# Attention scores taken on all 128 rows of TensorE, and three value tiles joined into one run, in a two-block transformer kernel

## The chip, the cores and the metric

One core of one Trainium2 chip runs the whole program. The metric is the time of one execution on the device in microseconds. The kernel before was run three times: 2970.2, 2977.2 and 2979.04 us, with a median of 2977.2 us.

## The reference

Two transformer layers of one sequence of 256 tokens and 2048 features, in float32. What matters here are the attentions, whose heads have 64 features, half of the 128 rows of the memories and of the product array.

```
# first block: chunked attention, 16 heads
scores = einsum('bcqhd,bckhd->bhcqk', qc, kb) * (hd ** -0.5)
p = softmax(scores + bias, masked)
out = einsum('bhcqk,bckhd->bcqhd', p, vb)

# second block: four mixers of 8 heads: (a) dilated, (b) window with sink and 2 shared KV heads,
#   (c) block selection, (d) native sparse attention: compressed + selected + window branches, gated
o_cmp = einsum('bhgqn,bhnd->bhgqd', softmax(q @ kc), vc)      # 15 compressed keys
```

Around them stand the projections `x @ w_in`, a memory attention (4 heads of 256 features), a convolution, feed-forward layers and a mixture of 16 experts.

## The kernel before

Activations lie with features on the 128 partitions and tokens along the row, in `pool`, 75 slots of 256 columns. A slot of queries or keys holds two heads: one on rows 0 to 63 and one on rows 64 to 127. All weights come as 1 MB tiles of 128 x 2048. Each tile passes four engines: SyncE issues its DMA into `raw`, ScalarE rounds it to float32r (`w_hi`, line 582), VectorE takes the rest (`w_lo`, line 1846), and TensorE multiplies it with split activations, three products for each pair of chunks (`three`, lines 1155 to 1157, or `both`, lines 1168 and 1169). Four tiles are in flight.

TensorE's stream is written out by hand: tile by tile, and in two places the attention of one head at a time is put between half tiles. Each such piece is a tick. At tick u, `attend` issues the scores of unit u (line 1361; 1358 for compressed keys; 1352 for memory heads), the transposes of the probabilities of unit u-3 (lines 1372 to 1378), and the value products of unit u-4 (lines 1391 to 1399). VectorE, ScalarE and GpSimd do the softmax of unit u in their own streams: VectorE adds the bias and takes the maximum (1932), ScalarE takes the exponential (714), VectorE the reciprocal (1958), GpSimd scales (2585), and after the transposes ScalarE copies them from PSUM to SBUF (730). TensorE waits for that copy before it transposes the next unit into the same PSUM bank. Local ticks lie in the stage called "glu", five to four tiles.

The second block's projections are the list `SECOND`: tiles of kind "rows" (output has features on the partitions), "cmp" (the weights of the key and value compression, 30 moved columns), "tokens" (values with tokens on the partitions, one 128-wide tile: products of 128 moved columns), "quad" (four tiles of values at once, products of 512 moved columns) and "out". `SLOT2` says which half of `psT` a tile sums into. `tick_half` places the units: 8 sink units, then 8 heads of native sparse attention with three units each (two causal, one compressed), then twice 8 causal heads. `idle_products` are products of ones that keep TensorE's clock up while it has to wait.

Of the kernel before, what the change touches and what calls it, by code (L numbers as in the profile page):

```python
# [207 lines left out]


def second_tiles():  # L210

    out = [("rows", K2 + 9, 1.0), ("rows", V2 + 8, 1.0), ("rows", Q2 + 4, 0.125), ("cmp", 0, 0),
           ("rows", Q2 + 5, 0.125), ("cmp", 1, 0), ("rows", Q2 + 6, 0.125), ("rows", Q2 + 7, 0.125),
           ("rows", K2 + 8, 1.0), ("tokens", V2 + 9, 1.0)]
    out += [("rows", Q2 + 12 + c, 0.125) for c in range(4)]
    out += [("rows", K2 + 10, 1.0), ("rows", K2 + 11, 1.0), ("tokens", V2 + 10, 1.0), ("tokens", V2 + 11, 1.0)]
# [9 lines left out]
def second_slots():  # L226

    out, at = [], 0
    for kind, _, c in SECOND:
        out.append(at)  # L230
        at = at if kind == "quad" and c < 3 else 1 - at
    return out
# [87 lines left out]
def build(nc, tiles, ada_tiles, x_d, mem_d, params_d, crow_d, rel_rev, onehot_d, maskrow_d, ident_d,  # L320
          cmpmask_d, tab_d, sinks_d, rbias_d, router_d, gd_d, w2_d, pe_d, grp_d, tri_d, out, fbias_d):
    with ExitStack() as ctx:
# [22 lines left out]
        ident = sb("ident", [P, P])  # L345
        small = sb("small", [P, 880])
        rstd = sb("rstd", [P, S])
# [98 lines left out]
        zero = col(1)  # L446
        kc_sb = col(NCMP)
        vc_sb = col(P)[0:NCMP, :]
        rb, grp = col(NE), col(NE)
# [125 lines left out]
        def _(act):  # L575
# [126 lines left out]
            def attend(units, at, scratch, ticks=None):  # L702
                n = len(units)
                for u in range(n + 3) if ticks is None else ticks:
# [15 lines left out]
                    if u >= 3:  # L720
                        v = u - 3
                        unit, slot = units[v], (at + v) % 2
                        act.wait_ge(W["probs_transposed"], at + v + 1)
                        wait(act, W["pv_ready"], at + v - 1)
                        dst = flat(scratch[1] + 2 * slot, 2)
                        if unit["kind"] == "cmp":
                            ins = nc.scalar.activation(dst[0:NCMP, 0:S], psP[0:NCMP, 0:S], ACT.Copy)
                        else:
                            w = 2 * S if unit["kind"] == "mem" else S + P
                            ins = nc.scalar.activation(dst[:, 0:w], psP[:, 0:w], ACT.Copy)  # L730
                        ins.then_inc(W["probs_copied"], 1)
# [52 lines left out]
            linear("k", HC, K, 1.0)  # L784
            token_major("v", V)
# [212 lines left out]
            for n, (kind, dest, x) in enumerate(SECOND):  # L998
# [19 lines left out]
                attend(SECOND_UNITS, 20, SC2, ticks_at(n, 0, N_UNITS + 3))  # L1018
                if kind in ("rows", "tokens"):
                    act.wait_ge(used, t.count())  # L1020
                    nc.scalar.activation(pool[:, dest, :], psT[:, SLOT2[n], 0:S], ACT.Copy, scale=x)\
                        .then_inc(emptied["A"], 1)
                elif kind == "quad" and x == 3:
                    token_sums(t + -3, SLOT2[n], dest)
# [113 lines left out]
        def _(pe):  # L1138
# [201 lines left out]
            def attend(units, at, scratch, q0, k0, v0, outs, ticks=None):  # L1340
                n = len(units)
                for u in range(n + 4) if ticks is None else ticks:
                    if u < n:
                        unit, slot = units[u], (at + u) % 2

                        mem = u >= 2 and units[u - 2]["kind"] == "mem"
                        wait(pe, W["exp_ready"] if mem else W["max_ready"], at + u - 1)
                        for qt in range(2):
                            dst = psS[:, slot, qt * S:qt * S + S]
                            if unit["kind"] == "mem":  # L1350
                                for c in range(2):
# [12 lines left out]
                    if 3 <= u < n + 3:  # L1364
# [4 lines left out]
                        for qt in range(2):  # L1369
                            p = pool[:, scratch[0] + 2 * ((at + v) % 4) + qt, :]  # L1370
                            if unit["kind"] == "cmp":
                                last = nc.tensor.transpose(psP[0:NCMP, qt * P:qt * P + P], p[:, 0:NCMP], ident[:, :])
                                continue
                            last = nc.tensor.transpose(psP[:, qt * P:qt * P + P], p[:, 0:P], ident[:, :])
                            if unit["kind"] == "mem":
# [4 lines left out]
                    if u >= 4:  # L1380
# [178 lines left out]
            def second_half(n, half):  # L1559

                kind, what, x = SECOND[n]
                t = Tile(BASE["two"] + n)
                slot = SLOT2[n]
                if half == 0:
                    pe.wait_ge(lo_done, t.count())
                    before = slot_before(n)
                    if before is not None and not (kind == "quad" and x):
                        who = OWN[BASE["two"] + before]
                        pe.wait_ge(emptied[who], OWN[:BASE["two"] + before + 1].count(who))
# [22 lines left out]
                else:  # L1592
                    tt = half
                    for k in range(DC if kind == "tokens" else 4):
                        if kind == "tokens":
                            dst, kk, at, width = psT[:, slot, tt * P:tt * P + P], k, k * P, P
                        else:
                            dst, kk, at, width = psT[:, slot, tt * 512:tt * 512 + 512], 4 * x + k, 512 * k, 512
                        xh, xl = a_hi[:, kk, tt * P:tt * P + P], a_lo[:, kk, tt * P:tt * P + P]
                        wh, wl = w_hi[:, t.k % SPL, at:at + width], w_lo[:, t.k % SPL, at:at + width]  # L1600
                        nc.tensor.matmul(dst, xh, wh, start=kk == 0, stop=False)
# [5 lines left out]
            def second_ticks(n, half):  # L1607
# [4 lines left out]
                for u in ticks_at(n, half, N_UNITS + 4):  # L1612
                    if u in (0, 8, 32, 40):
                        pe.wait_ge(emptied["A"], OWN[:BASE["two"] + {0: 10, 8: 18, 32: 30, 40: 42}[u]].count("A"))
                    attend(SECOND_UNITS, 20, SC2, Q2, K2, V2, 20, [u])
# [31 lines left out]
            run_sums("norm2")  # L1647
            idle_products(14)
            pe.wait_ge(W["router_lo"], 1)
# [184 lines left out]
        def _(dve):  # L1834
# [144 lines left out]
            nc.vector.memset(ones[:, :], 1.0).then_inc(W["ones_set"], 1)  # L1979
            nc.vector.memset(zero, 0.0).then_inc(W["ones_set"], 1)  # L1980
            nc.vector.memset(g8, -3.0e38)
            nc.vector.memset(w8, -3.0e38).then_inc(W["ones_set"], 1)
# [65 lines left out]
            for n in range(HC):  # L2048
# [4 lines left out]
                attend(MEM_UNITS, 0, SC1, QM, mem_ticks(n, 1, 8))  # L2053
            joined("k", 2 * HC, K, 1.0)
            others("v", HC)
# [272 lines left out]
            def cmp_ready(r):  # L2328

                dve.wait_ge(W["cmp_out"], r + 1)  # L2330
                if r == 0:
                    for j in range(2):
                        ins = nc.vector.tensor_copy(kc_sb[64 * j:64 * j + 64, :],
                                                    psP[64 * j:64 * j + 64, NCMP * j:NCMP * j + NCMP])
                else:
                    ins = nc.vector.tensor_copy(vc_sb, psP[0:NCMP, 0:P])
                ins.then_inc(W["cmp_ready"], 1)
# [373 lines left out]
def layout(a):  # L2711
# [61 lines left out]
    second = cut(np.concatenate([part[10], part[11], heads(part[3]), part[4], part[5], heads(part[9]), part[12],  # L2773
                                 part[14], part[13], part[15]], axis=1), 16, 1)
    second = np.concatenate([second[0:3], cut(a["nsa_cmp_w1_k_2"][0], 16, 1), second[3:4],
# [54 lines left out]
```

## Time and profile before

| | |
|---|---|
| median of three runs | 2977.2 us |
| the profiled execution | 2975.78 us |
| its span, first to last instruction | 2973.7 us |
| TensorE busy | 2912.3 us, 98% |
| VectorE busy | 2166.5 us, 73% |
| ScalarE busy | 1493.1 us, 50% |
| mean granted clock of TensorE | 0.991 |

TensorE is busy nearly throughout. Matmuls are pipelined and their ends are modelled: a product that takes 0.28 us in the profile is followed by the next after 0.12 us. The granted clock has two levels, 1 (2.4 GHz) and 0.5 (1.2 GHz).

### The profile page before, as it was taken

To read this page: it belongs to the slowest core of one execution; us is meant where nothing else is said; L and a number is where in the kernel's file an instruction comes from. 1 tells how busy PE (TensorE), PEld (TensorE's weight loads), DVE (VectorE), ACT (ScalarE), POOL (GpSimd) and SP (SyncE) were. 2 spreads that over 40 slices of the span, in tenths; PEclk is the share of its full clock that TensorE was granted. 3 is DMA by queue.
4 is the path that set the end of the run, shared out by engine and by line. 5 is a ranking of instruction groups with operands and counts; after the bars stand their busy time and mean duration, and the time that the engine had idled before them with its cause. 6 is when DMAs were issued, how large, how long until landed. Compare 5 with 4: busy or idle time off the path is not lost.

```text
span 2973.7 us, 46205 instructions
## 1 busy us (share of the span) xinstructions
PE 2912.3 (98%) x18218; PEld 2604.1 (88%) x18218; DVE 2166.5 (73%) x2651; ACT 1493.1 (50%) x1691; POOL 158.3 (5%) x228
## 2 busy tenths in 40 slices
PE   9999999999999999999999989999999999999998
PEld 8888788888888899999999989988989889889887
DVE  5644459999876999999999864455765876776874
ACT  5543554445554544444444444445545664664663
POOL 3000000000000000000000200111110000000001
PEclk9999999999999999999999989999999999999999
DMA  7545445555554988887788564344406895885882
GB/s 277 185 155 184 164 147 191 185 183 184 205 195 155 360 333 319 332 331 314 318 327 329 216 217 170 135 152 154 135 28 231 334 345 222 316 334 213 341 311 83
DMA packets 114816, 692.27 MB, mean 233 GB/s; under 512 B 14144, under 2 KB 27696, under 8 KB 33648
## 3 DMA queue, kind: packets, MB, share of 16 engines
q1 hardware_dynamic: 109088, 675.33, 60.2%
q10 hardware_dynamic: 4688, 11.01, 1.2%
q0 software_dynamic: 896, 3.93, 0.4%
q8 instruction: 100, 1.64, 0.2%
q14 instruction: 44, 0.36, 0.0%
HBM read 679.74 MB, written 10.49 MB: 232 GB/s over the span
## 4 chain that ended last, share of the span: by engine, by line
PE 89%; DVE 5%; ACT 3%; issue 1%; DMA 1%; POOL 0%; DVEq 0%; ACTq 0%; SPq 0%; POOLq 0%
PE psT L1168 22%; PE psT L1169 11%; PE psT L1155 6%; PE psT L1156 6%; PE psT L1157 6%; PE psT L1277 3%; PE psT L1732 3%; PE psT L1730 3%; PE psT L1731 3%; PE psT L1720 2%; PE psT L1721 2%; PE psT L1719 2%; DVE w_lo L1846 2%; PE psY L1771 1%; PE psY L1769 1%; PE psY L1770 1%
## 5 line engine op out<-in xcount | busy, mean ns | idle before, releaser
L1846 DVE TENSOR_TENSOR w_lo<-raw,w_hi 128x2048 fp32r<-128x2048 f32 x534 | 1225.1, 2298 | 395.2 <-ACT w_hi L582 391.3
L582 ACT ACTIVATE w_hi<-raw 128x2048 fp32r<-128x2048 f32 x534 | 1019.0, 1909 | 399.5 <-PE psT L1157 139.4
L1168 PE MATMUL psT<-a_both,w_hi 128*128 128x512 f32 x3072 | 1091.0, 400 | 9.9 <-DVE a_both L1896 2.8
L1169 PE MATMUL psT<-a_both,w_lo 128*128 128x256 f32 x3072 | 864.6, 281 | 0.0
L1168 PEld LDWEIGHTS psT<-a_both,w_hi 128*128 128x128 f32 x3072 | 579.0, 188 | 152.8 <-issue 9.9
L1169 PEld LDWEIGHTS psT<-a_both,w_lo 128*128 128x128 f32 x3072 | 582.9, 190 | 0.2
L1155 PE MATMUL psT<-a_both,w_hi 128*128 128x256 f32 x784 | 228.6, 292 | 8.3 <-DVE w_lo L1846 5.6
L1155 PE MATMUL psT<-h_hi,w_hi 128*128 128x256 f32 (+1 forms) x800 | 228.7, 286 | 4.9 <-DVE h_lo L2310 1.8
L1157 PE MATMUL psT<-h_hi,w_lo 128*128 128x256 f32 (+1 forms) x800 | 227.8, 285 | 0.0
L1156 PE MATMUL psT<-h_lo,w_hi 128*128 128x256 f32 (+1 forms) x800 | 227.7, 285 | 0.0
L1156 PE MATMUL psT<-a_both,w_hi 128*128 128x256 f32 x784 | 224.5, 286 | 0.0
L1157 PE MATMUL psT<-a_both,w_lo 128*128 128x256 f32 x784 | 224.1, 286 | 0.0
L2168 DVE CUSTOM_DVE_ANT_0 pool<-pool 128x2048 f32<-128x2048 f32 x96 | 219.4, 2285 | 5.2 <-DVE mod L2176 5.2
L1155 PEld LDWEIGHTS psT<-a_both,w_hi 128*128 128x128 f32 x784 | 152.8, 195 | 12.1 <-DVE w_lo L1846 6.3
L1155 PEld LDWEIGHTS psT<-h_hi,w_hi 128*128 128x128 f32 x800 | 155.5, 194 | 6.4 <-DVE w_lo L1846 2.0
L1157 PEld LDWEIGHTS psT<-h_hi,w_lo 128*128 128x128 f32 x800 | 155.7, 195 | 0.0
L1156 PEld LDWEIGHTS psT<-h_lo,w_hi 128*128 128x128 f32 x800 | 155.6, 195 | 0.1
L1156 PEld LDWEIGHTS psT<-a_both,w_hi 128*128 128x128 f32 x784 | 152.8, 195 | 0.1
L1157 PEld LDWEIGHTS psT<-a_both,w_lo 128*128 128x128 f32 x784 | 152.7, 195 | 0.0
L1730 PE MATMUL psT<-w_hi,xw_hi 128*128 128x512 f32 x384 | 151.0, 393 | 0.0
L1732 PE MATMUL psT<-w_hi,xw_lo 128*128 128x512 f32 x384 | 149.8, 390 | 0.0
L1731 PE MATMUL psT<-w_lo,xw_hi 128*128 128x512 f32 x384 | 149.7, 390 | 0.0
(358 smaller groups left out, 4618.8 us busy)
## 6 DMA issues: line engine op xcount, KB each, us to landing
raw<-tiles_dram SPq DMA_DIRECT2D x534, 1024.0 KB, 5.2
pool<-ada_tiles_dram SPq DMA_DIRECT2D x96, 1024.0 KB, 4.9
bias_rows_dram<-pool ACTq DMA_DIRECT2D x1, 8192.0 KB, 56.1
pool<-bias_rows_dram SPq DMA_DIRECT2D x40, 128.0 KB, 4.5
pool<-bias_rows_dram SPq DMA_DIRECT2D x40, 64.0 KB, 4.6
pool<-mem_dram SPq DMA_DIRECT2D x4, 512.0 KB, 9.9
pool<-x_dram ACTq DMA_DIRECT2D x1, 2048.0 KB, 11.6
pool<-x_dram POOLq DMA_DIRECT2D x1, 2048.0 KB, 10.0
```

The costliest lines, as they stand in the source:

```text
L582: nc.scalar.activation(w_hi[:, t.k % SPL, :], raw[:, t.k % RAW, :], ACT.Copy).then_inc(hi_done, 1)
L1155: nc.tensor.matmul(ps_out, wh, x_hi, start=first, stop=False)
L1156: nc.tensor.matmul(ps_out, wh, x_lo, start=False, stop=False)
L1157: return nc.tensor.matmul(ps_out, wl, x_hi, start=False, stop=last)
L1168: nc.tensor.matmul(dst.rearrange("p (h s) -> p h s", h=2), wh, a_both[:, :, a, :], start=first, stop=False)
L1169: return nc.tensor.matmul(dst[:, 0:S], wl, a_hi[:, a, :], start=False, stop=last)
L1277: nc.tensor.matmul(dst.rearrange("p (h s) -> p h s", h=2), w_hi[:, slot, at:at + P], a_both[:, :, a + k, :], start=k == 0, stop=False)
L1730: nc.tensor.matmul(dst, xw_hi[:, k, :], wh, start=k == 0, stop=False)
L1731: nc.tensor.matmul(dst, xw_hi[:, k, :], wl, start=False, stop=False)
L1732: last = nc.tensor.matmul(dst, xw_lo[:, k, :], wh, start=False, stop=k == DC - 1)
L1846: nc.vector.tensor_tensor(w_lo[:, t.k % SPL, :], raw[:, t.k % RAW, :], w_hi[:, t.k % SPL, :].bitcast(F32), ALU.subtract).then_inc(lo_done, 1)
L2168: nc.vector.tensor_tensor_reduce(out=buf, in0=buf, in1=flat(CROW, 8), scale=1.0, scalar=0.0, op0=ALU.mult, op1=ALU.add, accum_out=ada_acc[ ...
```

## The change

Every score product of a 64-feature head now takes all 128 rows. The moving operand, the keys, is kept twice: in one slot rows 64 to 127 are zeros, in its twin rows 0 to 63. The stationary operand is the whole slot of queries, both heads; the zeros of the keys remove the other head. `SECOND_KEYS` and `FIRST_TWINS` say where the twins lie. ScalarE writes both copies from PSUM, with a column of ones and zeros as scale; in the first block, where the sum comes in two halves, VectorE adds the second half to both. The compressed keys and values (15 of them) are padded with zeros to full rows; their probabilities are transposed and copied at full width.

The value tiles of the shared heads (one of the sink attention, two of native sparse attention) were three "tokens" tiles at places 9, 16 and 17 of the list. They are now three tiles "three" at places 9 to 11, laid out so that each of the 16 chunks moves 384 columns at once. A chunk that crosses the border of two weight tiles is cut in two. ScalarE copies the sums out once, after the third. TensorE waits for that copy before value products of the first sink unit (tick 4). Nine idle products are added before the first "cmp" tile, and six before the second block's router.

```diff
-                            r = 64 * unit["half"]
-                            q = pool[r:r + 64, q0 + unit["q"], qt * P:qt * P + P]
+                            q = pool[:, q0 + unit["q"], qt * P:qt * P + P]
                             if unit["kind"] == "cmp":
-                                last = nc.tensor.matmul(dst[:, 0:NCMP], q, kc_sb[r:r + 64, :], start=True, stop=True)
+                                last = nc.tensor.matmul(dst[:, 0:NCMP], q, keys_c[unit["half"]], start=True, stop=True)
                             else:
-                                last = nc.tensor.matmul(dst[:, 0:w], q, pool[r:r + 64, k0 + unit["k"], 0:w],
+                                last = nc.tensor.matmul(dst[:, 0:w], q, pool[:, key_place(unit), 0:w],
                                                         start=True, stop=True)
...
+                            last = nc.tensor.transpose(psP[:, qt * P:qt * P + P], p[:, 0:P], ident[:, :])
                             if unit["kind"] == "cmp":
-                                last = nc.tensor.transpose(psP[0:NCMP, qt * P:qt * P + P], p[:, 0:NCMP], ident[:, :])
                                 continue
...
-                            last = nc.tensor.matmul(psO[:, 0:S], vc_sb, pT[0:NCMP, 0:S], start=False, stop=True)
+                            last = nc.tensor.matmul(psO[:, 0:S], values_c, pT[:, 0:S], start=False, stop=True)
...
+                if n == 3 and half == 0:
+                    idle_products(9)
...
+                            left, right = max(0, 2048 * x - 384 * kk), min(384, 2048 * x + 2048 - 384 * kk)
+                            if left >= right:
+                                continue
+                            at = 384 * kk + left - 2048 * x
+                        dst = psT[:, slot, tt * 512 + left:tt * 512 + right]
...
-                    if u in (0, 8, 32, 40):
+                    if u in (0, 4, 8, 32, 40):
...
-            idle_products(14)
+            idle_products(20)
...
+                    if dest - K2 in SECOND_KEYS:
+                        nc.scalar.activation(pool[:, dest, :], sums, ACT.Identity, bias=zero, scale=upper_half)
+                        nc.scalar.activation(pool[:, SECOND_KEYS[dest - K2], :], sums, ACT.Identity, bias=zero,
+                                             scale=lower_half).then_inc(emptied["A"], 1)
...
+                    nc.vector.scalar_tensor_tensor(upper, psT[:, t.k % 2, 0:S], upper_half, upper, ALU.mult, ALU.add)
+                    nc.vector.scalar_tensor_tensor(lower, psT[:, t.k % 2, 0:S], lower_half, lower, ALU.mult, ALU.add)\
+                        .then_inc(emptied["D"], 1)
```

Two places of TensorE's stream show what is moved. The first is the border between the third query tile of the second block and the first "cmp" tile (`h_hi` and `h_lo` hold the compression's activations). Before:

```order
L1156 MATMUL psT<-a_both,w_hi 128x256
L1157 MATMUL psT<-a_both,w_lo 128x256
L1155 MATMUL psT<-h_hi,w_hi 128x30
L1156 MATMUL psT<-h_lo,w_hi 128x30
L1157 MATMUL psT<-h_hi,w_lo 128x30
```

After:

```order
L1185 MATMUL psT<-a_both,w_hi 128x256
L1186 MATMUL psT<-a_both,w_lo 128x256
L1171 MATMUL psY<-ones 128x128 x9
L1184 MATMUL psT<-h_hi,w_hi 128x30
L1185 MATMUL psT<-h_lo,w_hi 128x30
L1186 MATMUL psT<-h_hi,w_lo 128x30
```

Nine idle products now stand between the two tiles. The second place is the first value tile of the shared heads, of which the beginning stands here for before:

```order
L1156 MATMUL psT<-a_both,w_hi 128x256
L1157 MATMUL psT<-a_both,w_lo 128x256
L1601 MATMUL psT<-w_hi,a_both 128x128
L1602 MATMUL psT<-w_lo,a_both 128x128
L1603 MATMUL psT<-w_hi,a_both 128x128
```

And a piece of its middle, where the weight tile ends within a chunk and the second half of the tokens begins, for after:

```order
L1636 MATMUL psT<-w_hi,a_both 128x384
L1637 MATMUL psT<-w_lo,a_both 128x384
L1638 MATMUL psT<-w_hi,a_both 128x384
L1636 MATMUL psT<-w_hi,a_both 128x128
L1637 MATMUL psT<-w_lo,a_both 128x128
L1638 MATMUL psT<-w_hi,a_both 128x128
L1636 MATMUL psT<-w_hi,a_both 128x384
```

Each of the three tiles had 96 products of 128 columns. The run now has 84 products of 384 columns, 12 of 256 and 12 of 128 in all, and stands where the first of the tiles stood.

## Rows read from the trace of the kernel before

**Rows 1.** The page: busy time, share, instructions; chain that ended last, by engine.

```profile
PE 2912.3 (98%) x18218; PEld 2604.1 (88%) x18218; DVE 2166.5 (73%) x2651; ACT 1493.1 (50%) x1691; POOL 158.3 (5%) x228
...
PE 89%; DVE 5%; ACT 3%; issue 1%; DMA 1%; POOL 0%; DVEq 0%; ACTq 0%; SPq 0%; POOLq 0%
```

**Rows 2.** Waits of TensorE: total us, times, longest us.

```profile
PE psY L1374 <- ACT pool L730: 4.0, 4, 1.8
...
PE psT L1155 <- DVE h_lo L2310: 1.8, 1, 1.8
```

**Rows 3.** Timeline, memory heads: start us, us, engine, line, operation, count, [idle before].

```profile
186.48 0.28 PE L1169 MATMUL psT<-a_both,w_lo 128*128 128x256 f32 x1
186.60 1.89 PE L1352 MATMUL psY<-pool 128*128 128x256 f32 x8
188.32 0.27 PE L1374 MATMUL psY<-ident,pool 128*128 128x128 f32 x1
```

**Rows 4.** Timeline of TensorE, one sink unit of the second block.

```profile
1841.85 0.28 PE L1157 MATMUL psT<-a_both,w_lo 128*128 128x256 f32 x1
1842.06 0.92 PE L1361 MATMUL psY<-pool 64*128 64x128 f32 x4
1842.91 0.44 PE L1374 MATMUL psY<-ident,pool 128*128 128x128 f32 x2
...
1843.30 0.60 PE L1398 MATMUL psY<-pool 128*128 128x256 f32 x2
1843.73 0.39 PE L1399 MATMUL psY<-pool 128*128 128x128 f32 x2
...
1844.07 0.28 PE L1156 MATMUL psT<-a_both,w_hi 128*128 128x256 f32 x1
```

**Rows 5.** Timeline of TensorE: scores and transposes, then value products, of compression units.

```profile
1909.43 0.28 PE L1157 MATMUL psT<-a_both,w_lo 128*128 128x256 f32 x1
...
1910.41 0.60 PE L1398 MATMUL psY<-pool 128*128 128x256 f32 x2
...
1918.04 0.27 PE L1378 MATMUL psY<-ident,pool 128*128 128x128 f32 x1
1918.24 0.69 PE L1395 MATMUL psY<-pool,small 15*128 15x256 f32 x2
...
1919.09 0.28 PE L1156 MATMUL psT<-a_both,w_hi 128*128 128x256 f32 x1
```

**Rows 6.** A "tokens" tile (stretch: us, busy, clock, DMA share, GB/s); a "quad" tile, timeline.

```profile
1797.30:1808.10 10.80, 10.80 (x98) 10.69 (x96) 0.00 (x0) 0.38 (x1) 1.00 0.34 117
...
1948.55 0.39 PE L1603 MATMUL psT<-w_hi,a_both 128*128 128x512 f32 x1
...
1949.23 0.39 PE L1603 MATMUL psT<-w_hi,a_both 128*128 128x512 f32 x1
```

**Rows 7.** Timeline of TensorE: idle products before the second router.

```profile
2201.24 3.29 PE L1142 MATMUL psY<-ones 128*128 128x128 f32 x28
2206.03 0.28 PE L1534 MATMUL psY<-a_both,h_hi 128*16 128x256 f32 x1 [1.50 <-DVE a_both L1909]
```

**Rows 8.** Around the compression tiles: stretches (PE, PEld, DVE, ACT, POOL, clock, DMA); timeline.

```profile
1747.50:1753.00 5.50, 5.50 (x51) 5.50 (x49) 5.43 (x10) 0.38 (x1) 0.00 (x0) 0.97 1.02 368
1752.70:1756.00 3.30, 3.30 (x17) 3.30 (x17) 1.50 (x2) 1.91 (x1) 0.00 (x0) 0.50 1.01 420
...
1762.90:1776.50 13.60, 13.60 (x66) 13.60 (x66) 5.97 (x10) 2.29 (x3) 0.00 (x0) 0.50 1.02 387
...
1753.99 1.91 ACT L582 ACTIVATE w_hi<-raw 128x2048 fp32r<-128x2048 f32 x1 [5.93 <-DMA raw<-tiles_dram]
...
1755.93 2.29 DVE L1846 TENSOR_TENSOR w_lo<-raw,w_hi 128x2048 fp32r<-128x2048 f32 x1 [1.80 <-ACT w_hi L582]
```

**Rows 9.** Timeline in the first block: a ScalarE copy out of PSUM, a wait of TensorE.

```profile
416.39 0.37 ACT L793 ACTIVATE pool<-psT 128x256 f32<-128x256 f32 x1
...
416.63 0.41 PE L1374 MATMUL psY<-ident,pool 128*128 128x128 f32 x2 [1.45 <-ACT pool L730]
```

More of the change, by code:

```diff
@@ L207, with key_place @@
 Q2, K2, V2 = 0, 16, 48
+SECOND_KEYS = {0: 25, 1: 55, 2: 56, 3: 57, 4: 72, 5: 73, 6: 74, 7: 58, 8: 52, 10: 53, 11: 54}
+FIRST_KEYS, FIRST_TWINS = 16, 32
+def key_place(unit):
+    if unit["kind"] == "local":
+        return (FIRST_TWINS if unit["half"] else FIRST_KEYS) + unit["k"]
+    return SECOND_KEYS[unit["k"]] if unit["half"] else K2 + unit["k"]
 def second_tiles():
@@ L213, in second_tiles @@
            ("rows", Q2 + 5, 0.125), ("cmp", 1, 0), ("rows", Q2 + 6, 0.125), ("rows", Q2 + 7, 0.125),
-           ("rows", K2 + 8, 1.0), ("tokens", V2 + 9, 1.0)]
+           ("rows", K2 + 8, 1.0)] + [("three", V2 + 9, c) for c in range(3)]
     out += [("rows", Q2 + 12 + c, 0.125) for c in range(4)]
-    out += [("rows", K2 + 10, 1.0), ("rows", K2 + 11, 1.0), ("tokens", V2 + 10, 1.0), ("tokens", V2 + 11, 1.0)]
+    out += [("rows", K2 + 10, 1.0), ("rows", K2 + 11, 1.0)]
     for m, q in ((0, 0), (1, 8)):
@@ L230, in second_slots @@
         out.append(at)
-        at = at if kind == "quad" and c < 3 else 1 - at
+        at = at if (kind == "quad" and c < 3) or (kind == "three" and c < 2) else 1 - at
     return out
@@ L345, in build @@
         ident = sb("ident", [P, P])
-        small = sb("small", [P, 880])
+        small = sb("small", [P, 912])
         rstd = sb("rstd", [P, S])
@@ L446, in build @@
         zero = col(1)
[L447 to L448 removed]
+        keys_c = col(NCMP), col(NCMP)
+        values_c = col(P)
+        upper_half, lower_half = col(1), col(1)
         rb, grp = col(NE), col(NE)
@@ L725, in attend @@
                         dst = flat(scratch[1] + 2 * slot, 2)
[L726 to L730, printed above, removed]
+                        w = {"mem": 2 * S, "cmp": S}.get(unit["kind"], S + P)
+                        ins = nc.scalar.activation(dst[:, 0:w], psP[:, 0:w], ACT.Copy)
                         ins.then_inc(W["probs_copied"], 1)
@@ L783, in _ @@
                 attend(MEM_UNITS, 0, SC1, mem_ticks(n, 1, 7))
-            linear("k", HC, K, 1.0)
+            with act.Fori(0, HC // 4) as i:
+                for k in range(4):
+                    t = Tile(BASE["k"] + k, i, 4)
+                    split(t + AHEAD)
+                    src = lower_sums(t)
+                    nc.scalar.activation(pool[:, bass.ds(i * 4 + (K + k), 1), :], src, ACT.Identity, bias=zero,
+                                         scale=upper_half)
+                    nc.scalar.activation(pool[:, bass.ds(i * 4 + (KM + k), 1), :], src, ACT.Identity, bias=zero,
+                                         scale=lower_half).then_inc(W["lower_copied"], 1)
             token_major("v", V)
@@ L1018, in _ @@
                 attend(SECOND_UNITS, 20, SC2, ticks_at(n, 0, N_UNITS + 3))
-                if kind in ("rows", "tokens"):
+                if kind == "three" and x == 2:
                     act.wait_ge(used, t.count())
-                    nc.scalar.activation(pool[:, dest, :], psT[:, SLOT2[n], 0:S], ACT.Copy, scale=x)\
-                        .then_inc(emptied["A"], 1)
+                    for tt in range(2):
+                        ins = nc.scalar.activation(pool[:, dest:dest + 3, tt * P:tt * P + P],
+                                                   psT[:, SLOT2[n], tt * 512:tt * 512 + 384].rearrange("p (c s) -> p c s", c=3),
+                                                   ACT.Copy)
+                    ins.then_inc(emptied["A"], 3)
+                elif kind == "rows":
+                    act.wait_ge(used, t.count())
+                    sums = psT[:, SLOT2[n], 0:S]
+                    if dest - K2 in SECOND_KEYS:
+                        nc.scalar.activation(pool[:, dest, :], sums, ACT.Identity, bias=zero, scale=upper_half)
+                        nc.scalar.activation(pool[:, SECOND_KEYS[dest - K2], :], sums, ACT.Identity, bias=zero,
+                                             scale=lower_half).then_inc(emptied["A"], 1)
+                    else:
+                        nc.scalar.activation(pool[:, dest, :], sums, ACT.Copy, scale=x).then_inc(emptied["A"], 1)
                 elif kind == "quad" and x == 3:
@@ L1566, in second_half @@
                     before = slot_before(n)
-                    if before is not None and not (kind == "quad" and x):
+                    if before is not None and not (kind in ("quad", "three") and x):
                         who = OWN[BASE["two"] + before]
@@ L1980, in _ @@
             nc.vector.memset(zero, 0.0).then_inc(W["ones_set"], 1)
+            nc.vector.memset(keys_c[0], 0.0)
+            nc.vector.memset(keys_c[1], 0.0)
+            nc.vector.memset(values_c, 0.0)
+            for r in (0, 64):
+                nc.vector.memset(upper_half[r:r + 64, :], 0.0 if r else 1.0)
+                nc.vector.memset(lower_half[r:r + 64, :], 1.0 if r else 0.0)
             nc.vector.memset(g8, -3.0e38)
@@ L2053, in _ @@
                 attend(MEM_UNITS, 0, SC1, QM, mem_ticks(n, 1, 8))
-            joined("k", 2 * HC, K, 1.0)
+            with dve.Fori(0, HC // 4) as i:
+                for k in range(4):
+                    t = Tile(BASE["k"] + k, i, 4)
+                    lo(t + AHEAD)
+                    dve.wait_ge(W["lower_copied"], i * 4 + (2 * HC + k + 1))
+                    upper, lower = (pool[:, bass.ds(i * 4 + (at + k), 1), :] for at in (K, KM))
+                    nc.vector.scalar_tensor_tensor(upper, psT[:, t.k % 2, 0:S], upper_half, upper, ALU.mult, ALU.add)
+                    nc.vector.scalar_tensor_tensor(lower, psT[:, t.k % 2, 0:S], lower_half, lower, ALU.mult, ALU.add)\
+                        .then_inc(emptied["D"], 1)
             others("v", HC)
@@ L2771, in rows @@
         return w.reshape(D, -1)
-    second = cut(np.concatenate([part[10], part[11], heads(part[3]), part[4], part[5], heads(part[9]), part[12],
-                                 part[14], part[13], part[15]], axis=1), 16, 1)
+    values = np.concatenate([part[5], part[13], part[15]], axis=1).reshape(DC, P, 384).transpose(1, 0, 2)
+    second = np.concatenate([cut(np.concatenate([part[10], part[11], heads(part[3]), part[4]], axis=1), 16, 1),
+                             values.reshape(P, 3, 2048).transpose(1, 0, 2),
+                             cut(np.concatenate([heads(part[9]), part[12], part[14]], axis=1), 16, 1)])
     second = np.concatenate([second[0:3], cut(a["nsa_cmp_w1_k_2"][0], 16, 1), second[3:4],
```

18 lines of the change are left out of this document (9 added, 9 removed).

## The prediction

> **What bounds the kernel now.** I read the page first: TensorE is busy 98% of the span and carries 89% of the chain that ended last; no other engine reaches 6% of that chain [rows 1]. So an instruction taken from TensorE's stream shortens the kernel by what it holds that stream, unless TensorE then waits. The list of TensorE's waits came next: in all the span it waits 4.0 us, in four places, for ScalarE's copy of transposed probabilities (line 730), and 1.8 us once for `h_lo` of the second compression tile [rows 2]. The attention is thus almost free of waits, and "busy" there has to be read from the starts of products in the timeline, because the ends are modelled and overlap. I call the distance from one start to the next the step.
>
> **A normal step.** A float32r product of 256 moved columns steps 0.12 us (186.48 to 186.60), a float32 one of 256 columns on 128 rows 0.215 us (eight from 186.60 to 188.32), followed at once by the transposes [rows 3]. Those eight are the scores of the memory heads, whose features fill all 128 rows: they show what full rows cost, and that going from float32r to float32 and back into transposes costs nothing extra. A product of 128 columns steps 0.11 us (96 of them in the 10.80 us of one value tile) [rows 6]; I take this for float32 also, since the two value products and the next one after 1843.73 fit it.
>
> **What 64 rows cost.** One whole causal or sink unit of the second attention runs from the start of the last wide product (1841.85) to that of the second wide product after it (1844.07): 2.22 us [rows 4]. At normal steps the same instructions make 0.12 + four score products 0.65 (two of 128, two of 256 columns) + three transposes 0.33 + four value products 0.65 + 0.12 = 1.87 us. The excess, 0.35 us, sits at the two borders of the 64-row group: 0.21 instead of 0.12 us on entry, the four scores with the way out 0.85 instead of 0.65, and the rest in the first transpose. All of it is absent in the 128-row scores [rows 3]. There are 16 local and 40 causal or sink units: 56 x 0.35 = **19.6 us** less.
>
> **Compression units** (8) enter narrow forms twice. Scores and transposes: from 1909.43 to 1910.41 0.98 us against 0.12 + 4 x 0.11 + 2 x 0.11 = 0.78, 0.20 too many. Value product on 15 rows: 1918.04 to 1919.09 1.05 us against 0.11 + 0.43 + 0.12 = 0.66, 0.39 too many [rows 5]. With keys, transposes and values on full rows both go: 8 x 0.59 = **4.7 us**. The transposes now load 128 columns where they loaded 15; their weight loads lie behind other products, as those of the ordinary transposes do.
>
> Bounds of both terms: nothing, if the excess belongs to something that stays, and all 24.3 us. I take all, because the 128-row twin of the operation stands in the same trace.
>
> **The value run.** Three tiles of 96 products at 10.8 us each are 32.4 us [rows 6]. After the change there are 84 products of 384 columns and 12 each of 128 and 256. No product of 384 is in the trace; it must lie between 0.12 (256 columns) and 0.227 us (512 columns: 1948.55 to 1949.23 is three steps) [rows 3, 6]. I take the middle, 0.173, as the engine is paced by columns from 256 on. 84 x 0.173 + 12 x 0.11 + 12 x 0.12 = 17.3 us, so **15.1 us** less (10.6 to 19.6). ScalarE and VectorE need 1.91 and 2.29 us to prepare a tile [rows 8], well under the 5.8 us it will last, and the DMA share of 0.34 leaves the transfers slack [rows 6]. The copy out happens once for three tiles, and the sink units' first value product comes after four more ticks, so the new wait at tick 4 ends early.
>
> **Idle products.** Fourteen of them last from 2201.24 to 2204.53, 0.235 us each [rows 7]. Six more before the second router are 1.4 us, and there TensorE then waits 1.50 us anyway [rows 7]: nothing. Nine more before the first compression tile are 2.1 us on the path, but all behind them moves too, and 1.8 us of waiting for `h_lo` comes one tile later [rows 2]. That wait ends by a chain that doesn't hang on the delayed tile: ScalarE stood idle for 5.93 us for the tile that it splits at 1753.99, which it had from the DMA only then, and the share of the DMA engines is 1.0 in this stretch [rows 8]. So + 0.3 us. If that chain is late by the same 2.1 us, the cost is 2.1.
>
> **The clock.** After the 1.8 us wait the granted clock stands at half (0.50, 1.2 GHz) for 13.6 us, through the whole second compression tile and after; the first one ran at full clock and was followed by only 3.3 us of half clock [rows 8]. With the wait filled I expect a fall like the first one: some 10 us less at half speed, 5 us at most in time. The narrow tile may hold the clock down as before, so between 0 and 6.8 us; I take **4**.
>
> **What is added elsewhere.** ScalarE writes a second copy of every key tile, 19 of them, about 0.37 us each as its other copies out of PSUM [rows 9]; in the first key stage VectorE adds twice. Neither engine is the bound in these tiles. But ScalarE's copy of transposed probabilities stands behind them in its queue, and TensorE waits for it: at 416.63, 1.45 us [rows 9]. Where it waits now, the 0.35 us taken from a unit comes back as waiting. Four places now, perhaps four more: + 1.3 us. The memsets at the start are covered by the idle products there.
>
> Sum: - 19.6 - 4.7 - 15.1 - 4 + 0.3 + 1.3 = - 41.8 us. The profiled execution took 2975.8 us, 1.4 less than the median of the runs, 2977.2; that gives 2934 by the one and 2935 by the other. I say **2935 us**.
>
> **Rivals.**
> A. *The chain of the other engines takes half of it back.* Scores, maximum, exponential, reciprocal, scaling and transposes follow each other over three ticks, and ScalarE is in front of four waits already [rows 2, 9]. Against it: about nine in ten units have no wait. Half of 24.3 us lost gives 2947.
> B. *The borders stay*, because they belong to the change of type or to the identity's loads and not to rows: 2977.2 - 15.1 - 4 + 0.3 = 2958. The memory scores speak against it [rows 3]. The Trainium skill ("TensorEngine Tiling (Array Packing)", Key Properties) says that changing the array's tiling drains it; by that rule rows, not the type, are the cause, and rows 4 beside rows 3 agree with it.
> C. *More*: the half clock around the compression tiles goes altogether, and 384 columns step as little as 0.15: 2935 - 2.8 - 1.9 = 2930. This is inside my own range.
> D. *Slower.* A shorter TensorE stream outruns the chain at every third tick or so, and each wait brings a fall of the clock, as after the 1.8 us above [rows 8]. A wait of 1.8 and 3.3 us at half clock is 3.5 us. Twelve such places eat the gain; with twenty the kernel is at 2935 + 70 = 3005. Today two waits are that long. The gain per tick (0.35 us) is too small to make a wait of 1.8 out of none.
> E. *Full rows cost double.* The Trainium skill ("TensorE: Matmul & The Clock Gate", Why this matters for your kernels) advises to put products of few rows into different row groups, where they run at the same time; by it the halves of two heads could overlap now, and full rows give that up. This trace does not agree: both score products of a unit stand on the same 64 rows, and their steps are those of full rows. As a mechanism of this kernel, a score group twice as dear is 64 x 0.65 = 41.6 us more, which would cancel the gain: 2977. From rows 3 and 4 I give it 1%.
>
> **Chances.** Forecast with C 82% (own range 2927 to 2944), A 11%, B 4%, E 1%, D 1%, 1% for the rest. What a measurement can tell from no change is 0.3%, 9 us. Faster by more than that holds for the forecast, C, A and B: 0.97; within it 0.02; slower 0.01. The range has to take in the runs' own spread, 2970 to 2979, and reaches toward A: 2925 to 2948.
>
> **What would show it.** After the change: the distance over the same piece of a unit 1.87 instead of 2.22 us; the score line with 128 rows and its weight loads without idle time; a compression unit shorter by 0.59; three value tiles in 17 to 18 us; no wait for `h_lo` in front of the second compression tile, and a shorter half clock there; line 730's copy waited for at up to eight places, under 6 us in all. Wrong would be the first term if the borders persist with 128 rows, the second if 384 columns step like 512, the fourth if the half clock stays 13 us.

## The result: 2951.8 us, 24 us faster than before

| | before | after |
|---|---|---|
| median of the runs made together | 2975.5 us (4 runs) | 2951.8 us (4 runs, 2948.0 to 2956.0) |
| ratio, with its 95% interval | | 0.9922 [0.9906, 0.9938] |
| the profiled execution | 2975.8 us | 2948.0 us |
| its span | 2973.7 us | 2946.2 us |

The kernel is 0.8% faster. The four runs of the kernel after lie 8 us apart, so single microseconds between medians mean little. The forecast was 2935 us, 41.8 us less than before; 23.7 us came, and the time lies outside the range of 2925 to 2948.

The page of the kernel after, lines of the same kind as in [rows 1]:

```profile
PE 2877.6 (98%) x18068; PEld 2596.4 (88%) x18068; DVE 2168.8 (74%) x2666; ACT 1503.5 (51%) x1709; POOL 158.3 (5%) x228
...
PE 83%; DVE 7%; ACT 6%; issue 3%; DMA 1%; POOL 0%; SPq 0%; DVEq 0%; ACTq 0%; POOLq 0%
```

TensorE is still busy 98%, but its share of the chain fell from 89 to 83%, and VectorE, ScalarE and "issue" gained what it lost. A piece was taken out of TensorE's stream, and in places another chain now sets the end.

The borders of the 64-row group are gone. Timeline of TensorE in the kernel after, one sink unit (start us, us, engine, line, operation):

```profile
1827.74 0.28 PE L1186 MATMUL psT<-a_both,w_lo 128*128 128x256 f32 x1
1827.86 0.82 PE L1389 MATMUL psY<-pool 128*128 128x128 f32 x4
1828.51 0.38 PE L1399 MATMUL psY<-ident,pool 128*128 128x128 f32 x2
1828.73 0.27 PE L1405 MATMUL psY<-ident,pool 128*128 128x128 f32 x1
1828.84 0.60 PE L1425 MATMUL psY<-pool 128*128 128x256 f32 x2
1829.28 0.38 PE L1426 MATMUL psY<-pool 128*128 128x128 f32 x2
...
1829.62 0.28 PE L1185 MATMUL psT<-a_both,w_hi 128*128 128x256 f32 x1
```

From 1827.74 to 1829.62 it is 1.88 us where [rows 4] had 2.22: entry 0.12 us, the four scores 0.65, as forecast. With all products of the attention on 128 rows the surplus of 0.35 us went. The Trainium skill ("TensorEngine Tiling (Array Packing)", Key Properties) says that a change of tiling drains TensorE; this trace agrees with it.

The value run is as forecast too. Timeline of TensorE in the kernel after, eight steps of 384 columns in 1.39 us, 0.174 us each:

```profile
1799.83 0.33 PE L1636 MATMUL psT<-w_hi,a_both 128*128 128x384 f32 x1
...
1801.22 0.33 PE L1638 MATMUL psT<-w_hi,a_both 128*128 128x384 f32 x1
```

What was not forecast stands at the top of TensorE's waits in the kernel after (total us, times, longest us):

```profile
PE psY L1399 <- ACT pool L739: 13.8, 10, 2.7
...
PE psY L1399 <- POOL pool L2634: 3.9, 7, 0.8
```

Line 1399 is the transposes, 739 ScalarE's copy out of PSUM (730 before). It was 4.0 us in four places [rows 2]; now it is 17.7 us in seventeen, if the second row belongs to it. It does. Timeline around one of its seven places (line 726 is the exponential, 714 before):

```profile
1901.07 0.49 ACT L726 ACTIVATE pool<-pool,small 128x256 f32<-128x256 f32 x1
...
1901.56 0.47 ACT L739 ACTIVATE pool<-psY 128x384 f32<-128x384 f32 x1
...
1902.18 0.41 PE L1399 MATMUL psY<-ident,pool 128*128 128x128 f32 x2 [0.44 <-POOL pool L2634]
```

The copy ends at 1902.03 and the transpose starts at 1902.18. At all seventeen places the copy ends 0.14 or 0.15 us ahead of the transposes. GpSimd is named because its semaphore is the other one of that wait, but it was then scaling a later unit; the scaling that these transposes need had run at 1895.31.

In the kernel before there was a little room at such places. Timeline of the kernel before, the same place of the head before:

```profile
1909.32 0.47 ACT L730 ACTIVATE pool<-psY 128x384 f32<-128x384 f32 x1
...
1910.18 0.39 PE L1372 MATMUL psY<-ident,pool 128*15 128x128 f32 x2
```

The copy ended 0.39 us ahead, and 0.34 to 0.69 us ahead at the seven places together, that is 0.20 to 0.55 us more than where TensorE waits for it. The three units of a head were to get 1.29 us shorter, more than that room.

Stage by stage, from the starts of the products at the stages' borders (us; the last three columns are the kernel after with the changes of the experiments below):

| stage | before | after | forecast change | copy first | remainder late | same, bias first |
|---|---|---|---|---|---|---|
| local attention, 16 units | 127.5 | 128.2 | -5.6 | 123.7 | 140.1 | 116.2 |
| gates, no attention | 410.3 | 404.5 | 0 | 404.7 | 404.6 | 410.3 |
| compression tiles | 55.6 | 55.5 | -3.7 | 55.5 | 55.6 | 55.5 |
| value tiles and 8 units | 79.6 | 62.1 | -17.9 | 62.1 | 62.1 | 62.1 |
| next 24 units and the 8 compressed | 203.4 | 198.3 | -13.1 | 190.1 | 192.8 | 190.2 |
| last 8 units, to the experts | 155.0 | 158.3 | -2.8 | 152.6 | 161.7 | 154.8 |

The forecast changes are the prediction's terms laid on the stages: 0.35 us a unit, 0.59 a compressed one, 15.1 for the value run, and 3.7 for clock and idle products. The value stage came in full. The other three stages with units should have lost 21.5 us and lost 1.0: 5.1 in the long one, and the local and the last one grew. Of the 6.3, 8.0 and 6.1 us missing in the local, the long and the last one, new waits for line 739 are 5.4, 6.2 and 2.2. (By their scores two units of the long stage fall into the last one, 0.7 us of the forecast.) What is left in the last stage is of the size of what TensorE's clock cost in this execution: it stood at half for 16.6 us instead of 8.2, at most 4.2 us. The windows of the last stage, before and after (us, busy of TensorE, its loads, VectorE, ScalarE, GpSimd, clock, DMA share, GB/s):

```profile
2080.30:2235.30 155.00, 146.49 (x1116) 137.08 (x1114) 108.05 (x254) 76.84 (x132) 16.25 (x28) 0.97 0.26 93
```

```profile
2049.90:2208.20 158.30, 149.84 (x1127) 142.54 (x1125) 107.95 (x254) 77.82 (x131) 16.24 (x28) 0.95 0.26 90
```

The 5.7 us of the gates stage are luck (see the end).

### The profile page after: what moved, and what is told of

It reads as the page before. It is cut to its first block, busy times and chain, and to the rows that moved or that the text cites. A ratio compares the mean times of both kernels' runs of the same rounds, so it can differ in the third digit from the quotient of the medians.

```text
span 2946.2 us, 45953 instructions
## 1 busy us (share of the span) xinstructions
PE 2877.6 (98%) x18068; PEld 2596.4 (88%) x18068; DVE 2168.8 (74%) x2666; ACT 1503.5 (51%) x1709; POOL 158.3 (5%) x228
## 4 chain that ended last, share of the span: by engine, by line
PE 83%; DVE 7%; ACT 6%; issue 3%; DMA 1%; POOL 0%; SPq 0%; DVEq 0%; ACTq 0%; POOLq 0%
PE psT L1197 21%; PE psT L1198 11%; PE psT L1184 5%; PE psT L1186 5%; PE psT L1185 5%; PE psT L1765 3%; PE psT L1767 3%; PE psT L1766 3%; PE psT L1306 3%; ACT w_hi L594 2%; PE psT L1754 2%; PE psT L1756 2%; PE psT L1755 2%; DVE w_lo L1881 2%; PE psY L1805 1%
```

## The experiments

**Which half of the change falls short?** The kernel before with the score half alone (full rows, twins of the keys, padding of the compressed ones):

```diff
-                            q = pool[r:r + 64, q0 + unit["q"], qt * P:qt * P + P]
+                            q = pool[:, q0 + unit["q"], qt * P:qt * P + P]
...
-                                last = nc.tensor.matmul(dst[:, 0:w], q, pool[r:r + 64, k0 + unit["k"], 0:w],
+                                last = nc.tensor.matmul(dst[:, 0:w], q, pool[:, key_place(unit), 0:w],
```

> The kernel before with full-row scores, twins of the keys and full-width compression units alone; the three value tiles stay apart and no idle products are added. The borders are gone in the trace of the changed kernel (going into the scores 0.12 us, out of them 0.22 us), so by the forecast this alone is 24 us: 2951 us. Theory T (the time comes back as waiting for ScalarE's copy of the transposed probabilities, which stands behind the exponential of a later unit in ScalarE's stream): most of it returns, waits for the copy rise from 4 to some 15 us, the gain is 4 to 9 us: 2966 to 2971 us.

And with the value run alone:

```diff
-            ("rows", K2 + 8, 1.0), ("tokens", V2 + 9, 1.0)]
+            ("rows", K2 + 8, 1.0)] + [("three", V2 + 9, c) for c in range(3)]
```

> The kernel before with the value run of 384 columns alone. By the products seen in the changed kernel (steps of 0.174 us) 32.4 us become 17.4: 15 us less, 2960.5 us, with waits as before. If the run brings forward the sink units and so makes waits, the gain is under 12 us.

Measured: the scores alone 2969.66 us (2961.7 to 2978.5), ratio 0.9983 [0.9969, 0.9998], with before at 2975.26 in the same runs; the values alone 2958.07 us, 0.9949 [0.9931, 0.9967]. So 5.6 us from the scores and 17.2 from the values, 22.8 together, close to the 23.7 of the whole. The intervals are wide: 0.6 to 9 us for the scores, 10 to 21 for the values. By the medians the value half gives what was forecast and the score half a quarter of it. TensorE's waits in the kernel with the score half alone are nearly those of the kernel after:

```profile
PE psY L1392 <- ACT pool L739: 11.2, 10, 2.0
PE psY L1392 <- POOL pool L2619: 3.9, 7, 0.8
```

With the value half alone the wait for the copy (line 730 there) is little more than the 4.0 us of before:

```profile
PE psY L1381 <- ACT pool L730: 5.9, 6, 1.8
```

**Does the copy's place eat it?** In each tick ScalarE takes the exponential of unit u and then copies the transposed probabilities of unit u-3. The copy needs nothing of the exponential, but stands behind it, and the exponential waits for VectorE's maximum. The edit puts the copy first, in the kernel after and in the kernel before:

```diff
+                    if u >= 3:
+                        v = u - 3
+                        ...
+                        ins = nc.scalar.activation(dst[:, 0:w], psP[:, 0:w], ACT.Copy)
+                        ins.then_inc(W["probs_copied"], 1)
...
-                    if u >= 3:
-                        v = u - 3
-                        ...
-                        ins = nc.scalar.activation(dst[:, 0:w], psP[:, 0:w], ACT.Copy)
-                        ins.then_inc(W["probs_copied"], 1)
```

> The changed kernel; in each tick ScalarE copies the transposed probabilities of unit u-3 before it takes the exponential of unit u, instead of behind it. Theory T: TensorE's waits at the transposes (17.7 us in the changed kernel) fall under 4 us, the kernel is 12 to 18 us faster than the changed one: 2934 to 2940 us. Rival (what is missing lies in the clock or in dearer products, the waits only stand where TensorE would wait anyway): within 4 us of 2952.

> The same order of ScalarE in the kernel before. Theory T: only its own 4 us of waits can go, 2971 to 2974 us: the copy's place matters only once TensorE's borders are gone. Rival (the copy's place is worth the same in any kernel): 12 us or more, 2963 us or less.

Measured: after, 2935.29 us (2934.2 to 2941.1), ratio 0.9879 [0.9858, 0.9899], 16.5 less than the kernel after. Before, 2970.19 us, 0.9988 [0.9974, 1.0003]: 5 us by the medians, and not clear of nothing. The same edit is worth 16 us where the borders are gone and at most 8 where they are not: the borders were time in which the copy got done. TensorE's waits with the copy first, from the top:

```profile
PE psY L1425 <- DVE pool L2011: 5.3, 4, 2.0
PE psT L1184 <- DVE w_lo L1881: 4.6, 2, 4.4
PE psY L1729 <- DVE pool L2541: 3.8, 1, 3.8
```

Both rows of line 1399 are gone from the list, that of GpSimd too; a smaller wait, of the value products for VectorE's copy of a finished head, took over at four places.

**Was the size of the borders right?** The kernel with the score half alone, and the same move of the copy:

```diff
+                        ins.then_inc(W["probs_copied"], 1)
                     if u < n:
```

> Full-row scores and compression units alone (as e1), with ScalarE's copy ahead of the exponential. If the copy's place was all that ate the 24.3 us of the borders, this kernel is 20 to 26 us under the kernel before, 2949 to 2955 us, and 15 to 20 under e1 (2969.7). If the borders are worth less than worked out, it stays above 2958 us.

Measured: 2950.72 us (2948.0 to 2958.2), 0.9924 [0.9907, 0.9941] of 2975.71, that is 25.0 us, and 18.9 under the same kernel with the copy behind. Up to 5 of the 25 can be the copy's own. The table agrees: with the copy first the 24 and 8 units of the long stage lost 13.3 us, against 13.1 forecast. The terms of 19.6 and 4.7 were of the right size.

**The nine idle products and the clock.** First without them, then moved ahead of the second compression tile, both with the copy first:

```diff
-                if n == 3 and half == 0:
-                    idle_products(9)
```

> e3 (changed kernel with the copy first, 2935.3 us) without the nine idle products ahead of the first compression tile. Forecast's step (they fill the later wait and save half clock): 4 us slower, 2939. Now expected from the traces, where both stretches of half clock came as before: the nine cost nothing or up to 2 us, so 2933 to 2935.

```diff
-                if n == 3 and half == 0:
+                if n == 5 and half == 0:
                     idle_products(9)
```

> e3 with the nine idle products moved from ahead of the first compression tile to ahead of the second, where TensorE waited 1.8 us in the kernel before. If it is the filled wait that matters for the clock, the half clock behind it shortens and the kernel is 2 to 5 us faster than e3: 2931 us. If the narrow tile itself lowers the clock: 2934 to 2936 us.

Measured: without them 2933.17 us (2931.5 to 2937.5), 0.9861 [0.9842, 0.9879]; moved, 2935.35 us (2928.7 to 2941.8), 0.987 [0.9851, 0.9889]. Neither can be told from the 2935.29 with them in place. In the kernel after, the stretches around the two compression tiles (us, busy of TensorE, its loads, VectorE, ScalarE, GpSimd, clock, DMA share, GB/s) are:

```profile
1745.70:1752.40 6.70, 6.70 (x33) 6.70 (x33) 5.23 (x7) 5.39 (x4) 0.00 (x0) 0.50 1.02 424
1752.60:1759.20 6.60, 6.60 (x60) 6.60 (x59) 2.15 (x5) 2.42 (x4) 0.00 (x0) 1.00 1.03 424
1759.40:1769.50 10.10, 10.10 (x49) 10.10 (x49) 5.00 (x10) 2.03 (x2) 0.00 (x0) 0.50 1.01 311
```

The granted clock is at half for 6.8 and 10.2 us, some 17 in all. Before it was 3.4 and 13.7, again some 17 [rows 8]. No wait stood ahead of either stretch now: TensorE ran the narrow tile of 30 columns before both, a product each 0.11 us and without a gap. Timeline before the first:

```profile
1745.19 0.26 PE L1185 MATMUL psT<-h_lo,w_hi 128*128 128x30 f32 x1
...
1745.52 0.26 PE L1185 MATMUL psT<-h_lo,w_hi 128*128 128x30 f32 x1
```

So a wait is not needed for the clock to fall there.

How long the half clock lasts changes from one execution to the next. In the four profiled kernels with the nine products in their place the stage took 55.5 or 55.6 us. In the eight without them it took 55.1 to 55.6 us in four, with 17 us at half clock and a wait of 1.5 to 1.8 us for `h_lo`; 51.8 or 51.9 in three, with 13.6 us at half clock and no such wait; and 53.6 in one. With the products moved it took 52.3, with 10.2 us at half clock. One profile each doesn't tell what decides between them.

**The other end of the chain.** What holds the copy back begins at VectorE, which computes the weight remainder (line 1881, 2.29 us) ahead of the maximum of a unit in the middle of a tile. Timeline of the kernel after around the fifth of these waits:

```profile
376.79 2.29 DVE L1881 TENSOR_TENSOR w_lo<-raw,w_hi 128x2048 fp32r<-128x2048 f32 x1 [0.92 <-ACT w_hi L594]
...
378.66 0.82 PE L1389 MATMUL psY<-pool 128*128 128x128 f32 x4
378.99 0.28 DVE L1967 CUSTOM_DVE_ANT_0 pool<-psY,pool 128x128 f32<-128x128 f32 x1
...
379.99 0.40 ACT L726 ACTIVATE pool<-pool,small 128x128 f32<-128x128 f32 x1 [3.24 <-DVE small L1977]
...
380.88 0.47 ACT L739 ACTIVATE pool<-psY 128x384 f32<-128x384 f32 x1
...
381.50 0.41 PE L1399 MATMUL psY<-ident,pool 128*128 128x128 f32 x2 [2.02 <-ACT pool L739]
```

Remainder, maximum, exponential, copy, transposes, one behind the other without a gap. At all seventeen places ScalarE had stood idle for 1.9 us or more before the exponentials, and the copy came straight behind them; at sixteen the maximum came straight behind a remainder. The edit swaps the first two, with the copy left behind the exponential:

```diff
-                lo(t + AHEAD)
                 attend(LOCAL_UNITS, 4, SC1, Q, local_ticks(n, 0, 20))
+                lo(t + AHEAD)
```

(and in the second block, where a unit stands in the middle of the tile)

> The changed kernel with ScalarE's order as it is, but VectorE takes the maximum of the unit of a tile's first half before it splits the next weight tile (2.3 us), not behind it. Theory T with the whole chain (split, maximum, exponential, copy): the waits at the transposes fall as in e3, 2935 to 2942 us. If only the copy's own place in ScalarE's queue matters: 2950 to 2953.

Measured: 2964.10 us (2960.8 to 2979.9), ratio 0.9977 [0.9963, 0.999], 12 us slower than the kernel after: a clear miss of both expectations. TensorE's waits say only that the copy is later still, VectorE's say why:

```profile
PE psY L1399 <- ACT pool L739: 20.7, 8, 4.9
```

```profile
DVE pool L1967 <- DMA pool<-rel_rev_dram: 43.5, 9, 6.8
...
DVE pool L1967 <- DMA pool<-bias_rows_dram: 17.1, 6, 4.0
```

The kernel after has neither of the last two rows. The clock adds to the loss: in the local stage it stood at half for 17 us, against 3.4 in the kernel after. SyncE issues a weight tile's transfer only when the remainder has freed its buffer, and the biases of the next units stand behind that transfer in its queue. Timeline of the same kernel, VectorE and SyncE:

```profile
342.30 2.27 DVE L1881 TENSOR_TENSOR w_lo<-raw,w_hi 128x2048 fp32r<-128x2048 f32 x1
...
344.60 0.33 SPq L480 DMA_DIRECT2D raw<-tiles_dram  x1
...
344.97 4.94 SPq L486 DMA_DIRECT2D pool<-rel_rev_dram  x8
...
350.57 0.29 DVE L1967 CUSTOM_DVE_ANT_0 pool<-psY,pool 128x128 f32<-128x128 f32 x1 [5.03 <-DMA pool<-rel_rev_dram]
```

The remainder ends at 344.57, the tile's transfer is issued at 344.60, and the eight bias transfers take until 349.91 to issue. The next edit keeps the late remainder and puts the biases ahead of the tile on SyncE. A second kernel has the same order of transfers with the remainder in its old place and the copy first, where nothing should hang on them:

```diff
-                load_tile(Tile(BASE["glu"] + n))
...
                     load_bias(LOCAL_UNITS, u, 4, SC1)
+                load_tile(Tile(BASE["glu"] + n))
```

> The kernel after, with VectorE's weight remainder (line 1881) behind the maximum of the first-half unit, as in the run before, and with SyncE's bias transfers of a tile put ahead of that tile's weight transfer instead of behind it. Theory Q (the 12 us that the run with the remainder behind lost came from SyncE's queue: the weight transfer waits for the remainder to free its buffer, and the bias transfers of the next units stand behind it, so VectorE waited 60.6 us in 15 places for them): VectorE's waits for rel_rev_dram and bias_rows_dram fall from 60.6 us to under 5, TensorE's waits for line 739 from 20.7 to under 8, and the time is 2935 to 2946, below the kernel after. Rival (the later remainder is itself what TensorE or ScalarE waits for, and the late transfers are only beside it): TensorE's wait stays over 15 us and the time over 2955.

> The kernel after, with ScalarE's copy of the transposed probabilities ahead of the exponential, without the nine idle products, and with SyncE's bias transfers ahead of the weight transfer of their tile. VectorE never waits for bias transfers there (0.3 us in all with the copy first), so theory Q expects no difference from the same kernel with the old order of transfers, 2933: 2930 to 2938. If the weight transfers, issued up to 5 us later where eight bias transfers come first, become late for ScalarE, the time is over 2938 and ScalarE's idle time for the DMA of raw grows.

Measured: 2935.65 us (2933.0 to 2941.0), 0.9861 [0.9837, 0.9885], and 2935.95 us (2933.2 to 2942.9), 0.9856 [0.9831, 0.988]. In the first, VectorE has no row of waits for either bias tensor left, and line 739 costs TensorE 0.9 us, once:

```profile
PE psY L1399 <- ACT pool L739: 0.9, 1, 0.9
```

So the loss of the run before came from SyncE's queue: moving the bias transfers ahead gave 28 us back, the falls of the clock that came with the waits included. And the 16 us that the kernel after lacks can be had at either end of the chain. The order of transfers by itself, in the second of the two, changed nothing that can be measured (2935.95 against 2933.17 without it, ratios 0.9856 and 0.9861).

**All of it together**: copy first, late remainder with biases first, no nine idle products.

> The kernel after with all three edits: ScalarE's copy ahead of the exponential, VectorE's remainder behind the maximum with SyncE's bias transfers ahead of the weight transfer, and no nine idle products. The copy alone and the remainder with the transfers alone both gave 2935 to 2936, 16 us below the kernel after, and their stages of the second attention are equal to 0.1 us, so they remove the same waits there: theory: the gains don't add, except in the local stage, where the remainder behind the maximum gave 7.6 us more than the copy (116.2 against 123.7 us for 16 units). Expected 2926 to 2934, 2930. If the two gains add in full, it is 2920 or less; if the local stage's gain came by luck with the run's pace, 2933 to 2937.

Measured: 2934.32 us (2929.2 to 2938.3), 0.9855 [0.9838, 0.9872]. The gains don't add. The local stage is indeed shorter in its profile, 115.8 us against 123.7 with the copy first alone, but the gates stage behind it took 410.0 instead of 404.7, the slower of two paces told below. Whether the one has to do with the other stays open. The forecast of 2930 was missed by 4 us; the kernel before took 2979.25 us in the same runs and 2975.71 in those of two experiments earlier, so the 4 us can be the runs'. Six kernels now lie at 2933 to 2936, at ratios of 0.9855 to 0.9879 with intervals that overlap, and these runs can't rank them. All are 40 to 45 us below the kernel before in their own runs.

## Why the prediction missed

- **Borders, - 19.6 and - 4.7.** Right in size: 1.88 us a unit in the timeline where 1.87 was forecast, and 20 to 25 us in the kernel where little takes them back. In the kernel after a good half of them, 13.7 us in the profile, came back as waiting.
- **Chain and copies, + 1.3, "four places now, perhaps four more".** This is the step that failed. It was 17 places and 17.7 us, 13.7 more than before. The prediction named ScalarE's added copies of keys as the danger. They are not in the chain: at none of the 17 places does such a copy stand between the exponentials and the copy of probabilities. That copy stands behind the exponential, and where a unit stands in the middle of a tile that stands behind VectorE's 2.29 us remainder. What had to be read for each unit is how long before the transposes the copy ended; "about nine in ten units have no wait" counted waits and not margins. At seven places the margin was 0.34 to 0.69 us, too little for what the units ahead of it were to save.
- **Rival A** had this mechanism and took half of 24.3, 2947, with 11%. By the medians 5.6 of 24.3 us came from the score half alone, so some three quarters were lost. Its fraction was picked, not worked out.
- **Rival D** feared that each wait brings a fall of the clock. Waits came, up to 2.7 us long, and in the profiles the mean clock moved from 0.991 to 0.989. But the kernel before alone shows 0.988 to 0.992 in its runs, so that this can't be told from chance, and 3.4 us of the local stage are at half clock before and after. It did not make the kernel slower. In the run with the late remainder, with waits up to 4.9 us, the clock did fall with them. That no wait of 1.8 us could come out of none, because a tick gains only 0.35, was wrong: at two places where the kernel before had no wait the kernel after has one of 2.0 us.
- **Rivals B and E.** The borders went with the full rows, and a score group got cheaper, 0.65 us where 0.85 stood. Whether products on different rows could run at the same time no run tests: a unit's scores all stand on the same 64 rows, so that the trace of before says nothing on it, though the prediction read it as speaking against.
- **Value run, - 15.1.** Right: step 0.174 us (forecast 0.173), stage 14.6 us shorter in the kernel with this half alone, 17.2 by its medians. The wait at tick 4 did end early.
- **Clock, - 4.** Nothing came: some 17 us at half clock around the compression tiles before and after.
- **Idle products, + 0.3.** Near: the `h_lo` wait of 1.8 us is gone, the nine products hold 1.93 us, and the stage is 0.1 us shorter.
- **The sum.** With 13.7 us of new waits in place of 1.3, and 0 in place of - 4 for the clock, it is - 25.4 us; the medians give - 23.7. That they are so close is in part chance: the interval of the ratio leaves room for 18 to 28 us.

## What to carry to other kernels

Time taken out of the engine that bounds is kept only where the chain of the others has slack of that size at that place. So read for each unit when the thing that it needs was ready, and not only whether the profile shows a wait. An instruction that frees a buffer for the bounding engine belongs ahead of one that waits for something else in the same queue. And moving a producer by 2 us moves what hangs on the buffer it frees: here it was a transfer on SyncE, and the small transfers queued behind it.

## What the runs showed of the hardware

One stage has two paces. The gates stage of the table is 72 tiles of 32 products each, without attention. Over its first 48 tiles, which are identical, a tile takes 5.65 us in some executions and 5.55 in others. The same 200 us of the kernel before, and of the kernel after:

```profile
560.00:760.00 200.00, 200.00 (x1137) 173.87 (x1136) 177.70 (x239) 98.43 (x118) 18.85 (x10) 1.00 0.52 185
```

```profile
560.00:760.00 200.00, 200.00 (x1154) 175.11 (x1154) 179.73 (x242) 100.12 (x118) 18.87 (x10) 1.00 0.54 190
```

In these windows TensorE has no wait and no lower clock: 17 more products in the same time. The stage took 404.5 to 406.0 us in six profiles and 408.7 to 411.3 in seven, of thirteen kernels whose edits don't touch it. It is 5.7 us of the 27.5 between the spans of before and after, and not the change's; it may be part of the 8 us by which runs of one kernel spread. What sets the pace, the runs don't show.

And at the narrow tiles (30 moved columns) the granted clock falls to 1.2 GHz though TensorE has no gap, with idle products ahead of the tile or without: in the kernel with the products moved, it fell to 0.50 again at the second one. Stretches of that kernel:

```profile
1747.80:1751.00 3.20, 3.20 (x16) 3.20 (x16) 1.66 (x2) 1.91 (x1) 0.00 (x0) 0.50 1.01 420
1761.40:1768.00 6.60, 6.60 (x32) 6.60 (x33) 3.67 (x9) 2.03 (x2) 0.00 (x0) 0.50 1.00 406
```
